# Streaming encoder step on one core: query square sums from three bf16 parts, a remainder moved from GpSimd to VectorE, two selection rounds moved earlier

## What is computed

```python
x = x + 0.5 * swiglu(rms(x))             # w_gate, w_up: 2048 x 5504, w_down: 5504 x 2048
z = rms(x) @ w_in                        # queries, keys, values of head groups A, B and C, indexer of A
qb, qc, kc, ... = rms of each head       # q * rsqrt(mean(q*q) + eps) * gain, over 64 values of a head
x = x + concat(A, B, C) @ w_out          # A: attention to selected keys, B: window with sinks, C: chunk band
x = x + 0.5 * swiglu(rms(x))
```

## Time and profile before

| | |
|---|---|
| median of 3 runs | 2086.78 us |
| profiled execution, whole time | 2087.36 us |
| its span, first to last instruction | 2085.8 us |
| TensorE matmul busy | 2077.8 us, 100% |
| VectorE busy | 1171.3 us, 56% |
| ScalarE busy | 846.9 us, 41% |
| GpSimd busy | 91.5 us, 4% |
| granted TensorE clock | 1.00 |

### The profile page before, as it was taken

One profiled execution on the slowest core, in us unless ns is written; L12 is line 12 of the kernel. 1 busy time (PEld: TensorE's weight loads), 2 busy tenths in 40 slices (PEclk: granted clock), 3 DMA queues, 4 the chain that ended last, 5 costly groups with the idle time before them and its releaser, 6 DMA issues.

```text
span 2085.8 us, 41909 instructions
## 1 busy us (share of the span) xinstructions
PE 2077.8 (100%) x15817; PEld 2057.6 (99%) x15817; DVE 1171.3 (56%) x1788; ACT 846.9 (41%) x1290; POOL 91.5 (4%) x142
## 2 busy tenths in 40 slices
PE   9999999999999999999999999999999999999999
PEld 8999999999999999999999999999999999999999
DVE  7555445554455556588879755555445554455544
ACT  6333333333333344345668644333333333333332
POOL 1000000000000000022432000000000000000000
PEclk9999999999999999999999999999999999999999
DMA  7544545544544445544443454554545555545554
GB/s 255 162 161 157 170 160 166 169 160 159 169 159 166 165 154 173 180 140 156 150 149 111 146 163 162 166 169 160 170 157 165 166 165 161 168 161 163 165 181 140
DMA packets 101274, 339.96 MB, mean 163 GB/s; under 512 B 12149, under 2 KB 16293, under 8 KB 101200
## 3 DMA queue, kind: packets, MB, share of 16 engines
q1 hardware_dynamic: 95856, 329.41, 48.4%
q0 software_dynamic: 2960, 7.45, 1.3%
q10 hardware_dynamic: 2400, 2.33, 0.3%
HBM read 334.45 MB, written 5.28 MB: 163 GB/s over the span
## 4 chain that ended last, share of the span: by engine, by line
PE 97%; DVE 2%; ACT 0%; DMA 0%; issue 0%; SPq 0%; DVEq 0%; ACTq 0%
PE bank L603 32%; PE bank L605 31%; PE bank L604 31%; PE bank L690 1%; PE bank L723 1%; PE bank L705 1%; PE bank L667 0%; DVE w_lo L1376 0%; DMA raw<-in_w_ffn_gate 0%; PE bank L905 0%; DVE h_lo L1625 0%; PE bank L707 0%; DVE s_buf L1457 0%; ACT w_hi L1065 0%; DVE s_buf L1493 0%
## 5 line engine op out<-in xcount | busy, mean ns | idle before, releaser
L603 PE MATMUL bank<-h_hi,w_hi 128*128 128x288 f32 x3344 | 994.0, 297 | 3.1 <-DVE w_lo L1633 1.8
L604 PE MATMUL bank<-h_lo,w_hi 128*128 128x288 f32 x3344 | 986.4, 295 | 0.0
L605 PE MATMUL bank<-h_hi,w_lo 128*128 128x288 f32 x3344 | 983.2, 294 | 0.0
L1376 DVE TENSOR_TENSOR w_lo<-raw,w_hi 128x1024 fp32r<-128x1024 f32 x634 | 729.9, 1192 | 208.1 <-ACT w_hi L1065 207.5
L1065 ACT ACTIVATE w_hi<-raw 128x1024 fp32r<-128x1024 f32 x634 | 617.6, 1022 | 327.8 <-PE bank L605 327.0
L603 PEld LDWEIGHTS bank<-h_hi,w_hi 128*128 128x128 f32 x3344 | 626.5, 187 | 8.1 <-DVE w_lo L1633 2.9
L605 PEld LDWEIGHTS bank<-h_hi,w_lo 128*128 128x128 f32 x3344 | 629.6, 188 | 0.0
L604 PEld LDWEIGHTS bank<-h_lo,w_hi 128*128 128x128 f32 x3344 | 627.6, 188 | 0.2
L603 PE MATMUL bank<-gu_hi,w_hi 128*128 128x288 f32 x1376 | 407.0, 296 | 0.0
L604 PE MATMUL bank<-gu_lo,w_hi 128*128 128x288 f32 x1376 | 406.8, 296 | 0.0
L605 PE MATMUL bank<-gu_hi,w_lo 128*128 128x288 f32 x1376 | 406.4, 295 | 0.0
(11 more groups left out here) (203 smaller groups left out, 989.8 us busy)
## 6 DMA issues: line engine op xcount, KB each, us to landing
raw<-in_w_ffn_gate SPq DMA_DIRECT2D x168, 512.0 KB, 4.5
raw<-in_w_ffn_up SPq DMA_DIRECT2D x168, 512.0 KB, 4.6
raw<-in_w_ffn_down SPq DMA_DIRECT2D x96, 512.0 KB, 3.7
raw<-in_w_in SPq DMA_DIRECT2D x74, 512.0 KB, 4.7
raw<-in_w_ffn_down SPq DMA_DIRECT2D x64, 384.0 KB, 4.2
raw<-in_w_out SPq DMA_DIRECT2D x32, 512.0 KB, 4.6
raw<-in_w_ffn_down SPq DMA_DIRECT2D x32, 448.0 KB, 4.4
bias_rev<-bias_vectors POOLq DMA_DIRECT2D x11, 256.0 KB, 4.5
```

Source lines behind the costliest of these rows:

```text
L603: pe.matmul(out, w_hi[b][:, k, :], hi, start=(k == first_k), stop=False)
L604: pe.matmul(out, w_hi[b][:, k, :], lo, start=False, stop=False)
L605: mm = pe.matmul(out, w_lo[b][:, k, :], hi, start=False, stop=(k == last_k))
L1376: dve.tensor_tensor(w_lo[b][:, k, :], raw_tile(ph, j, s)[:, k, :], w_hi[b][:, k, :].bitcast(F32), ALU.subtract)\
```

## The change

It has four parts.

1. **Query squares of the cb bodies in three bf16 parts.** ScalarE now squares the query twice, once in float32 and once rounded to bf16 (`query_first_part`). GpSimd subtracts the bf16 part from the float32 squares, ScalarE rounds the rest to bf16 (`query_second_part`), and GpSimd subtracts again into a third bf16 part (`query_third_part`). `set_sums` multiplies each part with a bf16 matrix of 1/64: 18 bf16 products in place of 6 float32 ones. Five `set_sums` are changed, and those of phase a stay as they are. The six parts share memory with `o_hi`, and six small clears of their borders are added on GpSimd in prep.
2. **First pair.** `POOL_PIECES` is gone, and VectorE makes all nine pieces of w_lo.
3. **Selection.** Rounds 0 and 1 of `top_keys(2, ...)` are made in step 14, the last strip of cb's first body. Rounds 2, 3 and 4 stand one each in the second, third and fourth part of body 1, where before rounds 0, then 1 and 2, then 3 and 4 stood.
4. **End.** Twelve small bf16 products behind the last strip are removed.

```diff
-        POOL_PIECES = (4, 7)
...
-            14: [("s",)],
+            14: [("s",), ("t", 2, 0, 2)],
...
                         c = NT + scale_col(p, r)
-                        mm = pe.matmul(misc_bank(m)[:, c:c + 2], sq_wide[1 + p][:, FULL[r]], mean_hd2[:, :], start=True, stop=True)
+                        if keys:
+                            for i in range(3):
+                                mm = pe.matmul(misc_bank(m)[:, c:c + 2], sq_part[p][i][:, FULL[r]], mean_hd2_short[:, :],
+                                               start=(i == 0), stop=(i == 2))
+                        else:
+                            mm = pe.matmul(misc_bank(m)[:, c:c + 2], sq_wide[1 + p][:, FULL[r]], mean_hd2[:, :], start=True, stop=True)
...
+            def query_first_part(b, p):
+
+                act.wait_ge(evac, b * 4 + (phase["cb"].n0 + 2 + p))
+                act.activation(sq_set[1 + p], z_q[p][:, :], ACT.Square)
+                act.activation(sq_part[p][0][:, 0:NT], z_q[p][:, :], ACT.Square).then_inc(q_first, 1)
+
+            def query_second_part(b, p):
+
+                act.wait_ge(q_rest, b * 2 + (p + 1))
+                act.activation(sq_part[p][1][:, 0:NT], sq_set[1 + p], ACT.Copy).then_inc(q_second, 1)
...
+                        if j == 2:
+                            query_first_part(body + 1, 0)
...
-                    split(splits[j])
+                    if j == 2:
+                        query_second_part(body + 1, 0)
+                        query_first_part(body + 1, 1)
+                        split(splits[j], (0,))
+                        query_second_part(body + 1, 1)
+                        split(splits[j], (1,))
+                    else:
+                        split(splits[j])
...
-                if i not in POOL_PIECES:
-                    first_piece(i)
+                first_piece(i)
...
-                        late = {1: (2, 0, 1), 2: (2, 1, 3), 3: (2, 3, 5)} if isinstance(i, int) and i == 1 else {}
+                        late = {j: (2, j + 1, j + 2) for j in (1, 2, 3)} if isinstance(i, int) and i == 1 else {}
...
+            def query_third_part(b, p):
+
+                pool.wait_ge(q_second, b * 2 + (p + 1))
+                settled()
+                pool.tensor_tensor(sq_part[p][2][:, 0:NT], sq_set[1 + p], sq_part[p][1][:, 0:NT], ALU.subtract).then_inc(set_sq, 1)
+                pool.wait_ge(set_sq, set_squares(b, 1 + p))
+                settled()
...
-                square(z, 1 + p, n_done, number)
+                if n_done is None:
+                    pool.wait_ge(q_first, b * 2 + (p + 1))
+                    settled()
+                    pool.tensor_tensor(sq_set[1 + p], sq_set[1 + p], sq_part[p][0][:, 0:NT], ALU.subtract).then_inc(q_rest, 1)
+                    pool.wait_ge(q_rest, b * 2 + (p + 1))
+                    settled()
+                else:
+                    square(z, 1 + p, n_done, number)
...
-                    place_q(b, 0, b * 4 + (cb.n0 + 2), set_squares(b, 1), 4)
-                    place_q(b, 1, b * 4 + (cb.n0 + 3), set_squares(b, 2), 2)
+                    place_q(b, 0, None, None, 4)
+                    query_third_part(b, 0)
+                    place_q(b, 1, None, None, 2)
+                    query_third_part(b, 1)
```

More of the change, by code:

```diff
@@ L14 @@
 F32R = mybir.dt.float32r
+BF16 = mybir.dt.bfloat16
 P = 128
@@ L154, in encoder_step @@
             gu_lo = sb("gu_lo", [P, thirds[0], NT], F32R, ffn_scope)
+        with ExitStack() as scope:
+            sq_parts = sb("sq_parts", [P, 6, T_P + P], BF16, scope)
         o_hi = sb("o_hi", [P, 16, NT], F32R)
@@ L183, in encoder_step @@
         q_wide = [sb(f"q_n{s}", [P, WIDE]) for s in range(2)]
+        sq_part = [[sq_parts[:, 3 * p + i, :] for i in range(3)] for p in range(2)]
+        mean_hd2_short = sb("mean_hd2_short", [P, 2], BF16)
         with ExitStack() as scope:
@@ L254, in encoder_step @@
         consts = sem("constants_built")
+        part_pads = sem("square_parts_borders_cleared")
         pads_rdy = sem("unused_rows_and_columns_cleared")
@@ L261, in encoder_step @@
         first_lo = sem("first_pair_piece_lo_ready")
-        first_lo_pool = sem("second_strip_piece_lo_by_gpsimd_ready")
         second_hi = sem("second_pair_first_quarter_hi_ready")
@@ L284, in encoder_step @@
         kinv_rdy = sem("key_inverse_norm_ready")
+        q_first = sem("query_squares_and_first_part_ready")
+        q_rest = sem("query_squares_less_first_part_ready")
+        q_second = sem("query_squares_second_part_ready")
         scale_rdy = sem("query_scales_ready")
@@ L325, in x_piece @@
             return [at for at, (s, _) in enumerate(FIRST) if s == 0].index(i)
-        POOL_PIECES = (4, 7)
         def first_no(i):
             return sum(k.stop < DT for _, k in FIRST[:i + 1])
-        def first_lo_no(i):
-            return sum(k.stop < DT for at, (_, k) in enumerate(FIRST[:i + 1]) if at not in POOL_PIECES)
         def early_bank(n):
@@ L531, in load @@
                     sp.wait_ge(lo_rdy, (n - 3) * 2)
-                    if n == 5:
-                        sp.wait_ge(first_lo_pool, len(POOL_PIECES))
                 elif not (isinstance(n, int) and n < 4):
@@ L925, in first_pair @@
                         t5_vectors()
-                    if i in POOL_PIECES:
-                        pe.wait_ge(first_lo_pool, POOL_PIECES.index(i) + 1)
-                    elif ks.stop < DT:
-                        pe.wait_ge(first_lo, first_lo_no(i))
+                    if ks.stop < DT:
+                        pe.wait_ge(first_lo, first_no(i))
                     else:
@@ L1002, in _ @@
                     last_bodies()
-            plain = ident[:, :].bitcast(mybir.dt.bfloat16)
-            for _ in range(8):
-                pe.matmul(psum[7][:, 0:2], plain[:, 0:P], plain[:, 0:2], start=True, stop=True)
-            for _ in range(4):
-                pe.matmul(psum[6][0:HD, 0:2], plain[:, 0:HD], plain[:, 0:2], start=True, stop=True)
         def v_place(name):
@@ L1333, in _ @@
                         split(following(ph, t // 2, t % 2))
+                        if t == 3:
+                            query_second_part(0, 1)
                         prep_items(11 + t)
+                        if t == 1:
+                            query_first_part(0, 0)
+                        if t == 2:
+                            query_second_part(0, 0)
+                            query_first_part(0, 1)
                     def body(i, ph=ph):
@@ L1612, in _ @@
                                 (mean_hd[0:HD, 0:HD], 1.0 / HD), (mean_hd2[:, :], 0.0), (mean_hd2[0:HD, 0:1], 1.0 / HD),
-                                (mean_hd2[HD:P, 1:2], 1.0 / HD)):
+                                (mean_hd2[HD:P, 1:2], 1.0 / HD), (mean_hd2_short[:, :], 0.0),
+                                (mean_hd2_short[0:HD, 0:1], 1.0 / HD), (mean_hd2_short[HD:P, 1:2], 1.0 / HD)):
                 link(dve.memset(tile, value))
@@ L1826, in settled @@
                 pool.sem_inc(pool_passed, 1)
-            for done, i in enumerate(POOL_PIECES):
-                s, k = FIRST[i]
-                pool.wait_ge(first_hi, first_no(i))
-                pool.tensor_tensor(w_lo[s][:, k, :], raw[s][:, k, :], w_hi[s][:, k, :].bitcast(F32), ALU.subtract)\
-                    .then_inc(first_lo_pool, 1)
-                pool.wait_ge(first_lo_pool, done + 1)
             pool.wait_ge(hlo_rdy, DT)
@@ L1936, in _ @@
             pool.wait_ge(evac, prep.n0 + 1)
+            for part in (part for pair in sq_part for part in pair):
+                pool.memset(part[:, NT:WIDE], 0.0).then_inc(part_pads, 1)
+            pool.wait_ge(part_pads, 6)
             load_bias("c", 0, 0, 0)
@@ L1945, in _ @@
                 if step == 13:
-                    place_q(0, 0, cb.n0 + 2, set_squares(0, 1), 4)
+                    place_q(0, 0, None, None, 4)
                 if step == 14:
-                    place_q(0, 1, cb.n0 + 3, set_squares(0, 2), 2)
+                    query_third_part(0, 0)
+                    place_q(0, 1, None, None, 2)
+                    query_third_part(0, 1)
                 for it in PREP_ITEMS[step]:
```

## The result

| | before | changed |
|---|---|---|
| median of 5 runs each, side by side | 2086.78 us (2085.85 to 2088.17) | 2097.37 us (2095.81 to 2099.82) |
| profiled execution, span | 2085.8 us | 2095.8 us |
| mean granted TensorE clock | 1.00 | 0.997 |

A forecast was written before the change was run, and what follows sets the result against it. The prediction took TensorE's matmuls, filling 2077.8 of 2085.8 us, as the bound. Bodies +5.4, step 14 -0.65, start -1.27 and the rest 0 gave +3.5 us, 2090.3 us, range 2084.6 to 2095.5.

The forecast's parts named there:

- Part 1b: Attention bodies: TensorE waits in set_sums for the last third part; bodies 2 to 4 lose 1.5 us each, body 1 0.9.
- the 5.4 us of the bodies: Forecast loss summed over attention bodies 1 to 4: 1.5 us each in 2, 3 and 4, 0.9 in body 1.
- w: TensorE's wait in a body's set_sums for the last third part of the query squares, forecast at 2.1 us.
- the restart of 0.1: Extra 0.1 us allowed for TensorE's first products behind the wait in a body's set_sums.
- Part 1a: Products in set_sums: 18 bf16 ones cost 0.65 us, so each set_sums gains 0.61 to 0.67 us.
- the hand-over at about 0.1 us before the recorded end: In the bodies, a blocked GpSimd instruction gets going 0.1 us before the VectorE subtraction's end; the later alternative adds 1.6 us.
- Step 14: Last strip of cb's first body: no wait in set_sums, a gain of 0.65 us.
- Part 2: Start, all w_lo pieces on VectorE: waits for GpSimd go, piece 7 starts at 19.2 or 19.3, gain 1.27 us.
- Parts 3 and 4: Selection rounds moved and end products removed: selection counted as 0, the end gains nothing, at most 0.1 us.
- Blocking does not add up: Rival, 20%: in the bodies GpSimd gets in early between the split's halves, wait 0.5 us, bodies even: 2085.2 us.
- ready in time: Rival, 7%: in the bodies the ScalarE and GpSimd chain is 0.5 us shorter, TensorE never waits: 2081.7 us.
- One blocking more: Rival, 15%: in the bodies another GpSimd step falls under VectorE, wait 3.3 us, decides from 2.3: 2095.1 us.

The follow-up runs named there:

- e3_fill: The changed kernel with 42 unused bf16 products on TensorE ahead of set_sums in bodies 1 to 4: 2091.52 us, ratio 1.0019.
- e6_slow_squares: The kernel before, float32 products kept, with five unused GpSimd products ahead of the second query's square in bodies 1 to 4: 2106.03 us, ratio 1.0089.
- e1_start: The kernel before with only the start's edit, VectorE making all nine pieces of w_lo: 2085.88 us, ratio 0.9993.
- e8_rest: The kernel before with the changed start, selection and end, but float32 products kept: 2085.23 us, ratio 0.9989.
- e2_parts: The kernel before with the three bf16 parts of the query squares alone: 2100.68 us, ratio 1.0062.
- e9_woven: The changed kernel with set_sums split around the second pair's outputs, and out_lo and step 14's z_v read between w_lo halves: 2084.30 us, ratio 0.9984.
- e4_hold: The changed kernel with VectorE's w_lo of the third part held back until GpSimd's last third part is written: 2100.87 us, ratio 1.0066.
- e10_lo_early: The changed kernel with VectorE making out_lo between the two w_lo halves of the third part: 2091.23 us, ratio 1.0018.
- e5_late_sums: The changed kernel with set_sums of the attention bodies moved behind the second pair's outputs: 2094.31 us, ratio 1.0033.

## Why the prediction was wrong

The step that failed is the sum of Part 1b, "a loss of 1.5 us a body". It priced the wait at its own length. The chain behind it was right: GpSimd stands under both w_lo halves, and up to the second pair's outputs the four bodies lose 5.4 us, the table's 0.95 + 1.37 + 1.39 + 1.72. What the step left out is that TensorE's clock falls after such a stand. That costs another 1.5 us in each body, 6.0 in all; `e3_fill` took just this away, and `e6_slow_squares` made it without the change. The trace of before had no stand of that length once TensorE was busy: the longest were 1.0 us at the start and 0.6 us in the bodies, and its clock was 1.00. It could not show the price. Another execution could: in `e1_start` the same 0.6 us was followed by a fall. The Trainium skill ("TensorE: Matmul & The Clock Gate", section "HAM oscillation — how this bites in real kernels") describes a kernel that falls back to half speed after each of its waits and recommends keeping TensorE fed. The four falls to 0.50 agree in kind. The waits of that kernel are given as about 3 to 5 us, longer than the 2 us here, so the page does not say that these would be followed by a fall; the runs do. It should have been a rival of its own.

That the 5.4 us of the bodies came out exactly is partly luck. Counted as the prediction counts it, from where the key products could have started to where they did, w is 2.40, 2.15, 2.17 and 2.51 us, 0.2 more than 2.1 on average (the waits of the trace are shorter because they begin at the end of the turning). From the key products to the second pair's outputs it takes 1.20 us in place of the forecast's 1.41, and this makes up for it: the restart of 0.1 was not needed on top of the 0.36 for the key products, and the 18 products were 0.12 cheaper.

*Part 1a.* Right in place, the cost set a little high: 18 products take 0.53 us, not 0.65.

*Part 1b, the blocking.* The trace of VectorE and GpSimd in body 2 answers to the earlier trace rows:

```profile
1010.33 1.35 DVE L1401 TENSOR_TENSOR w_lo<-raw,w_hi 128x1024 fp32r<-128x1024 f32 x1 [0.43 <-ACT w_hi L1063]
...
1010.90 1.16 POOL L1921 TENSOR_SCALAR q_n<-z_q,qk_cols 128x288 f32<-128x288 f32 x1 [0.30 <-POOL z_prep L1912]
...
1012.06 1.23 DVE L1401 TENSOR_TENSOR w_lo<-raw,w_hi 128x1024 fp32r<-128x1024 f32 x1 [0.38 <-ACT w_hi L1063]
...
1012.34 1.54 POOL L1902 TENSOR_TENSOR sq_parts<-z_prep,sq_parts 128x288 bf16<-128x288 f32 x1 [0.28 <-POOL q_n L1921]
```

The scaled query, 0.51 us long by itself, takes 1.16, and the third part, 0.73 by itself, takes 1.54. Both end their own length after a point 0.12 to 0.14 us before VectorE's recorded end (1012.06 - 0.50 = 1011.56 against 1011.68; 1013.88 - 0.73 = 1013.15 against 1013.29). So the hand-over at about 0.1 us before the recorded end, which the forecast took, holds for these subtractions. The later one, about 115 ns after the end, which the Trainium skill ("SBUF — State Buffer", section "A bandwidth-pool intuition that's wrong (but worth ruling out)") gives for GpSimd writing the descriptors of a DMA beside a VectorE copy, does not.

*Step 14.* I took a gain of 0.65; it lost 0.16. There was no wait in `set_sums`, but the next strip waits 0.75 us for z_v, one of the signs that the prediction named for being wrong. VectorE reads z_v behind both w_lo halves of the split:

```profile
939.83 2.35 DVE L1401 TENSOR_TENSOR w_lo<-raw,w_hi 128x1024 fp32r<-128x1024 f32 x2
942.10 0.45 DVE L1425 TENSOR_TENSOR z_v<-bank,rstd 128x288 f32<-128x288 f32 x1
```

It ends at 942.55, and L603 starts at 942.60. Before, the longer float32 products hid this read. But that is only half of the account. Before, the read starts 0.44 us after `set_sums` (942.99 against 942.55), and 0.44 and 0.43 us after in `e1_start` and `e8_rest`; with the bf16 parts it starts 1.12 us after (942.10 against 940.98), and 1.14 in `e2_parts`. At its old place it would have ended at 941.87, just when the 18 products were done. So VectorE is 0.7 us later, and GpSimd's new subtractions are why. The mask of the selection in step 12, before:

```profile
931.43 0.29 DVE L1607 TENSOR_SCALAR a_mask<-idx_acc 128x256 f32<-128x256 f32 x1
```

In the changed kernel it stands beside the first subtraction of query 0:

```profile
929.75 0.74 POOL L1912 TENSOR_TENSOR z_prep<-z_prep,sq_parts 128x288 f32<-128x288 f32 x1 [2.06 <-ACT sq_parts L1175]
...
929.77 0.87 DVE L1632 TENSOR_SCALAR a_mask<-idx_acc 128x256 f32<-128x256 f32 x1
```

The mask of step 13 takes 0.41 us in place of 0.23, beside the last third part. The prediction looked for GpSimd standing behind VectorE here and found none, since VectorE makes no w_lo then; it did not look the other way round. In `e9_woven` the read stands one half earlier and L603 starts at 941.67.

*Part 2.* The start gained 1.57 us against 1.27, with no wait for GpSimd. Piece 7 started at 18.75 where I had 19.2. VectorE's new pieces took the 0.60 us each of my estimate (12.77 to 13.37, 13.80 to 14.40). It came to the first of them at 12.77 and not 13.26, mostly because the w_lo before it already started at 10.87 in that execution, at 11.27 in the trace of before and at 11.54 in that of `e1_start`, which gained only 1.0. So this term differs by half a us between executions, and that it came out above the forecast is at least in part luck.

*Parts 3 and 4.* Right as far as shown: `e8_rest` gained with both in it, and the wait of body 1 for `out_lo` is gone. Neither was run by itself.

*The rivals.* "Blocking does not add up" falls with the rows above, and "ready in time" with it. "One blocking more" gave 2095.1 us, near the result, for the wrong reason. By the start-to-start count w did pass its mark of 2.3 in bodies 1 and 4, yet the GpSimd rows there are those of body 2 (scaled query 1.15 us, last third part 1.54) and no further instruction is held up; ScalarE's second part of query 0 only came 0.2 to 0.3 us later. The chance of slower, 0.15 and a third of 0.58, is 0.34 and not 0.36.

## What to carry to other kernels

Price a stand of TensorE in a busy stretch as its length plus a possible fall to half clock behind it: here 1.5 us behind nearly every stand of 2 us, and behind some of 0.6 to 1.4. Look at the granted clock in windows behind every new wait. The mean of the span looks harmless (0.997), but its third decimal counts the falls, in executions without a trace as well. Filler products take the price away, and so does real work if it fills the wait. Before shortening work on the bounding engine, list what each other engine was finishing under it, and what new work on a third engine delays it: the read of z_v and `out_lo` were each hidden by just the products that were shortened or moved. A cure that holds one engine back (`e4_hold`) only helps if nothing urgent is queued behind it.

## What the runs showed of the hardware

- The place of the slow products need not show the cause. In the changed kernel the clock fell 2.1 to 2.4 us after TensorE had gone on. This delay is not fixed: it was 0.6 us in `e1_start`, 0.7 to 2.0 in `e6_slow_squares`, up to 2.5 in `e2_parts`, and in body 1 of `e2_parts` and `e4_hold` the clock fell before TensorE went on.
- The length of the stand alone does not decide it. All twelve stands of 1.90 to 2.64 us in the changed kernel, `e2_parts` and `e6_slow_squares` came with a fall. But one of 0.60 us was followed by one (`e1_start`) and the same stand in the trace of before was not; one of 1.09 us was and another was not (`e10_lo_early`); two of 1.48 us and one of 2.50 us were not (`e5_late_sums`). What else decides was not settled here.
- GpSimd and VectorE hold each other up both ways: GpSimd's third part takes 1.54 us beside a w_lo subtraction and 0.73 alone, and VectorE's mask of 0.29 us takes 0.87 beside GpSimd's subtraction.
- A fall lasted 3.4 us or twice that, and with products of 128x288 cost 1.5 us for each 3.4: at half clock three of them are 0.72 us apart and not twice 0.40.
- 18 bf16 products of two columns with a new stationary operand each take 0.53 us, 29 ns apiece, against 105 for a float32 record of the same width.
